# Two transformer blocks on one core: feature-form matmul slots taken apart into two halves of 256 tokens

## What is computed

```python
(gq, gk, gv, ga, gz, dq, dk, dv, iq, ik, iw, dz, xq, xz, gates) = split_cols(h @ w_in[i])
y_gla = gla_mixer(gq, gk, gv, ga, gz, w_gla_a_up[i], b_gla_a[i], g_gla[i])
y_dsa = dsa_mixer(dq, dk, dv, iq, ik, iw, dz, rel_bias)
y_mem = cross_mixer(xq, xz, rmsnorm(mem, g_mem[i]), w_mem_kv[i])
...
merged = (s_gla * (y_gla @ w_gla_out[i]) + s_dsa * (y_dsa @ w_dsa_out[i])
          + s_mem * (y_mem @ w_x_out[i]))
x = x + rmsnorm(merged @ w_o[i], g_post[i])
...
def swiglu(h, w_in, w_out):
    gate, up = jnp.split(h @ w_in, 2, axis=-1)
    return (jax.nn.silu(gate) * up) @ w_out
```

## Time and profile before

| | us |
|---|---|
| median of 3 runs | 2159.78 |
| lowest and highest | 2156.92, 2160.94 |
| the profiled execution | 2168.24 |
| its span, first to last instruction | 2166.4 |
| TensorE busy, matmuls | 2070.3 (96%) |
| TensorE busy, weight loads | 1719.5 (79%) |
| VectorE busy | 901.3 (42%) |
| ScalarE busy | 800.5 (37%) |

### The profile page before, as it was taken

One profiled execution on the slowest core, in us unless ns is written; L12 is line 12 of the kernel. 1 busy time (PEld: TensorE's weight loads), 2 busy tenths in 40 slices (PEclk: granted clock), 3 DMA queues, 4 the chain that ended last, 5 costly groups with the idle time before them and its releaser, 6 DMA issues.

```text
span 2166.4 us, 24460 instructions
## 1 busy us (share of the span) xinstructions
PE 2070.3 (96%) x10536; PEld 1719.5 (79%) x10536; DVE 901.3 (42%) x1071; ACT 800.5 (37%) x1112; POOL 11.9 (1%) x22
## 2 busy tenths in 40 slices
PE   7999999899999999999979999999898799999998
PEld 5798888778888688789867888888797577888887
DVE  3366265554243233533355333322656643333323
ACT  4442232443233332444454233322535733323321
POOL 0000000000000000000000000000000000000000
PEclk9999999999999999999999999999998999999999
DMA  5422122212233122332212222233231012222332
GB/s 182 128 79 75 42 83 93 78 59 97 97 139 114 39 98 98 104 108 79 73 45 88 97 97 97 84 110 101 85 117 59 1 67 79 97 97 97 97 97 78
DMA packets 33673, 192.43 MB, mean 89 GB/s; under 512 B 3689, under 2 KB 3817, under 8 KB 16818
## 3 DMA queue, kind: packets, MB, share of 16 engines
q1 hardware_dynamic: 30418, 180.15, 23.5%
q0 software_dynamic: 3168, 11.01, 1.9%
HBM read 187.35 MB, written 3.67 MB: 88 GB/s over the span
## 4 chain that ended last, share of the span: by engine, by line
PE 87%; DVE 7%; ACT 4%; issue 1%; DMA 1%; SPq 0%; DVEq 0%; ACTq 0%
PE PS L442 26%; PE PS L443 26%; PE PS L444 26%; DVE wlo L1443 1%; ACT whi L993 1%; DVE X L1503 1%; PE PS L962 1%; PE PS L625 1%; PE PS L611 1%; PE PS L977 1%; DMA raw<-in_stream 1%; ACT xp L1146 1%; PE PS L743 0%; PE PS L587 0%; ACT slg L1418 0%
## 5 line engine op out<-in xcount | busy, mean ns | idle before, releaser
L442 PE MATMUL PS<-hhi,whi 128*128 128x512 f32 x1416 | 561.4, 396 | 9.7 <-DVE hlo L1473 8.0
L443 PE MATMUL PS<-hlo,whi 128*128 128x512 f32 x1416 | 559.4, 395 | 0.0
L444 PE MATMUL PS<-hhi,wlo 128*128 128x512 f32 x1416 | 558.4, 394 | 0.0
L1443 DVE TENSOR_TENSOR wlo<-raw,whi 128x2048 fp32r<-128x2048 f32 x123 | 281.9, 2292 | 640.4 <-ACT whi L993 640.1
L993 ACT ACTIVATE whi<-raw 128x2048 fp32r<-128x2048 f32 x167 | 319.0, 1910 | 334.2 <-PE PS L444 333.4
L442 PEld LDWEIGHTS PS<-hhi,whi 128*128 128x128 f32 x1416 | 267.9, 189 | 74.3 <-issue 9.6
L444 PEld LDWEIGHTS PS<-hhi,wlo 128*128 128x128 f32 x1416 | 267.8, 189 | 59.7
L443 PEld LDWEIGHTS PS<-hlo,whi 128*128 128x128 f32 x1416 | 268.1, 189 | 59.1
L443 PE MATMUL PS<-wlo,ahi 128*128 128x512 f32 x352 | 139.0, 395 | 0.0
L444 PE MATMUL PS<-whi,alo 128*128 128x512 f32 x352 | 139.0, 395 | 0.0
L442 PE MATMUL PS<-whi,ahi 128*128 128x512 f32 x352 | 138.9, 395 | 0.0
(11 more groups left out here) (351 smaller groups left out, 2837.7 us busy)
## 6 DMA issues: line engine op xcount, KB each, us to landing
raw<-in_stream SPq DMA_DIRECT2D x167, 1024.0 KB, 4.8
gpost<-in_gposts POOLq DMA_DIRECT2D x5, 512.0 KB, 4.2
X<-in_x SPq DMA_DIRECT2D x4, 512.0 KB, 8.7
X<-in_x POOLq DMA_DIRECT2D x1, 2048.0 KB, 7.9
out<-X SPq DMA_DIRECT2D x4, 512.0 KB, 2.6
bias_line<-linet POOLq DMA_DIRECT2D x1, 1536.0 KB, 35.5
tbias<-bias_line POOLq DMA_DIRECT2D x1, 1024.0 KB, 7.4
memx<-in_mem POOLq DMA_DIRECT2D x1, 1024.0 KB, 9.7
```

The lines of the kernel that those rows point to most:

```text
L442: nc.tensor.matmul(out, lh, rh, start=(k == 0), stop=False)
L443: nc.tensor.matmul(out, lh, rl, start=False, stop=False)
L444: return nc.tensor.matmul(out, ll, rh, start=False, stop=(k == n_k - 1))
L1443: V_.tensor_tensor(wlo[:, s % 2], raw[:, s % 2], whi[:, s % 2], ALU.subtract).then_inc(lo_ready[s % 2], 1)
```

## The change

Each column group of a feature-form slot is gone through twice: first all 8 row blocks over tokens 0 to 255, into the left half of the group's PSUM bank, then all 8 over tokens 256 to 511, into the right half. Both the general helper and the feed-forward's loop are changed. Each matmul has 256 columns, the stationary tiles are loaded for both halves, and a slot has 96 matmuls in place of 48. Where `tokens` is 256 (the memory slots) there is one half, and nothing changes. The waits of `arrival` are in the left pass of the first group alone; in the loop the test for the wait is the old one, so that it stands in both passes. Token form and `wide_out` are not touched. The other engines' programs stay as they are.

```diff
-                    for i, k in enumerate(row_order(m) if arrival is normed else range(KT)):
-                        if arrival and g == 0:
-                            arrival(i)
-                        last = three(PS[:, 2 * (m % 2) + g, 0:tokens], i, KT,
-                                     (whi[:, p, k, c:c + P], wlo[:, p, k, c:c + P]), (hi[:, k, :], lo[:, k, :]))
+                    for t0 in range(0, tokens, C):
+                        ts = slice(t0, t0 + C)
+                        for i, k in enumerate(row_order(m) if arrival is normed else range(KT)):
+                            if arrival and g == 0 and t0 == 0:
+                                arrival(i)
+                            last = three(PS[:, 2 * (m % 2) + g, ts], i, KT,
+                                         (whi[:, p, k, c:c + P], wlo[:, p, k, c:c + P]), (hi[:, k, ts], lo[:, k, ts]))
...
-                        for j in range(2):
+                        for j, ts in itertools.product(range(2), (slice(0, C), slice(C, T))):
                             for at_, k in enumerate(order):
                                 if p == a and j == 0 and at_ >= 2:
                                     pe.wait_ge(S["hlo_ready"], h0 + at_ - 1)
-                                last = three(PS[:, 2 * g + j, :], at_, KT,
+                                last = three(PS[:, 2 * g + j, ts], at_, KT,
                                              (whi[:, p, k, j * P:j * P + P], wlo[:, p, k, j * P:j * P + P]),
-                                             (hhi[:, k, :], hlo[:, k, :]))
+                                             (hhi[:, k, ts], hlo[:, k, ts]))
```

More of the change, by code:

```diff
@@ L14 @@
+import itertools
 import math
```

## The result

The changed kernel takes 2186.7 us in the median of 4 runs, against 2160.4 for the kernel before: a ratio of 1.0127 with a 95% interval of 1.0106 to 1.0148, +26.4 us. The forecast was 2190, with slower at 0.76.

The account below looks back on a forecast made before the run. TensorE, busy 96% of the span, was taken as the bound. Slow pace +27 and arrival waits +3 gave +30 us on the 2159.8 median: 2190, range 2152 to 2202 (the forecast's own range 2180 to 2198).

Parts of the forecast that it names:

- Count starts, not durations: TensorE matmuls: durations overlap, so cost is the distance of two starts; durations at face value would give over 800 us.
- Slow everywhere, +27: All feature-form matmuls: halves at the slow pace, 235.6 ns a pair against 228.9 or 233.3 for one whole, +27 us.
- The choice of the memory slots' rows over the token form's: Memory keys, feature form with 256 tokens, had 117.8 ns; token form showed both paces; so the slow one was taken.
- Arrival waits, +3: First column groups after a turned norm: halved, TensorE must wait for VectorE's row blocks; together +3 us (2 to 5).
- rival 1: Each stretch's pace is set by how it begins and stays what it was: 2158, no measurable change; chance 0.15.
- rival 2: All halved feature-form matmuls run at the quick pace: -16 + 3 = -13 us, 2147, faster; chance 0.10.
- rival 3: Half of the halved matmuls slow, half quick: -16 and +27 averaged, +3, 2168; chance 0.10.
- rival 4: Feed-forward loop's doubled body of 192 matmuls is fetched again on each jump: +20 to +40 on the forecast; chance 0.07.
- Rival 5: A fixed price of 2.3 ns per added matmul: +11 us, with +3 for the arrivals 2174; chance 0.08.

Follow-up runs that it names:

- the run with half loads: Changed kernel with the feed-forward loop's stationary tiles cut to 64 columns, half of the gate and up outputs left out: 116.7 ns from start to start.
- the second profile: The kernel before, unedited, once more under the profiler: span 2161.9 us, both feed-forward stretches quick.
- the runs with other places: Changed kernel and kernel before, each with some slots' 128 stationary columns taken from other places among the 256; one execution each, paces flipped in some slots.
- slot 31: Slot with its stationary tiles started at column 16, 64 bytes on, in the kernel before and the changed kernel: 226.9 ns whole, 120.0 over halves.

## Why the prediction came out right, step by step

- **Count starts, not durations.** Held. The durations would have given over 800 us.
- **Slow everywhere, +27.** Right in its pace: some 8950 of 9744 matmuls at 117.8. The choice of the memory slots' rows over the token form's was the step that made the forecast, and it held in nine slots of ten. Its reason was weaker than I wrote it. In the run with the output weights in one piece the memory keys themselves ran at 113.3, so the form leans to the slow pace and isn't tied to it. Nothing in the prediction said why one form should be slow and the other quick, and nothing here does: in that the step was lucky. The base was mis-sized: 1224 slow matmuls before were one execution's draw. By the other, with 270 slow ones, the term is 4602 x 6.7 + 270 x 2.3 = +31.
- **Arrival waits, +3.** The four first groups behind a turned norm took 7.1, 5.6, 5.6 and 7.2 us before and 7.5, 7.2, 7.1 and 7.0 after, 3.3 more in all, 0.6 of it the pace. The size was right. The cause held in part: at the full clock the waits do give the forecast 7.2 us (7.24 in the run with half loads), but in this execution the group started at the lower clock in layer A and in the first feed-forward. In the second feed-forward, for which I had put 0 because it would start at the lower clock, it had the full one and waited, and the time came out the same. That these add up to the same 3 us is luck.
- **What I did not have.** The forecast for the two terms, with the base of the second profile, would be +34. I laid the changed kernel's trace beside that profile, matmul by matmul. The feature-form slots, first groups included, take 29.5 us more: of the missing 4.5, 2.5 are the matmuls that stayed at 113.3, and 1.7 one slot that stood in part at the lower clock in before. All other stretches together take 8.4 us less, though their instructions are the same, and the first matmul starts 0.4 later: 21.5 in all, as the two spans differ (21.6). (The medians differ by 26.4; executions of one kernel differ by several us.) The 8.4 stand where the changed kernel has less time at the lower clock: over the whole span 59 us of it, against 74 and 76 in the two profiles of before. Ten us of before's are at one place, the end of the linear attention's last tile. Window 235:275, before and then after:

```profile
235.00:275.00 40.00, 39.65 (x197) 34.62 (x196) 7.13 (x10) 12.77 (x12) 0.00 (x0) 0.87 0.15 52
```

```profile
235.00:275.00 40.00, 39.66 (x343) 39.60 (x343) 10.52 (x12) 14.10 (x14) 0.00 (x0) 1.00 0.16 53
```

The granted clock is 0.87 here in eight of the nine profiles whose general slots are whole, and 1.00 in four of the five whose slots are halved. Here the small matmuls took 3.1 us less in the changed kernel, and 1.0, 1.5, 1.2 and 1.1 us less in four more stretches. So +26 came out near +30 because two errors cancel: a base taken too slow, and a gain by the clock that I had put at nothing. Why the clock holds there wasn't settled: one profile of each kind goes the other way.
- **Rivals.** The starting pace kept (rival 1), all quick (rival 2) and half and half (rival 3) fell with the windows and the count of the changed kernel; the loop's body (rival 4) with the run of the loop alone. Rival 5, a fixed price for each matmul, isn't decided: the half-load runs would put it at 5.0 ns, over the 2.3 that I priced it at, and 4872 x 5.0 is +24, near what was measured; but with full loads the price went with the pace, and by the runs with other places it would be 13.3.

## What to carry to other kernels

Where TensorE is the bound, cost a matmul by the distance of starts in a row of the same form, at the same place of the operands, and look at several stretches, since one program can have two paces. A matmul split in two cost 2.3 to 6.7 ns more here in most stretches even with every load hidden, and one split to below 256 columns with full loads pays for the load, and here stayed at the lower clock as well. Before an order or a shape is tuned for the last per cent, try the placement in SBUF: moving the weights by 64 bytes (and what lies behind them by 256) gained 0.7% here, half of what the whole change had cost.

## What was not expected of the hardware

- The distance of starts depends on where the operands lie. At the old place of the weights two paces, 228.9 or 233.3 ns for 512 columns and 113.3 or 117.8 for 256, changing without a pause and lasting up to 250 us; 64 bytes on, one pace, 226.7 and 120.0 (slot 31, and the whole kernel). What in the two operands' addresses makes it is open.
- With 128 columns streamed against loads of 128 columns the granted clock stayed at 0.50 for some 900 us of a stream without idle time; with loads of 64 columns it was 1.00. The cause is open.
- At the lower clock that stream had 213 ns from start to start, the same as 256 columns streamed at that clock.
